# Moving a recurrence channel's gate-weight load behind its first four weight tiles in SP's transfer queue

## What is computed

```python
def even_layer(x, norm_pre, norm_post, w_in, conv_w, conv_b, gate_w, gate_b, lam, sc_w, w_out):
    h = rmsnorm(x, norm_pre)
    proj = h @ w_in
    xa, za, xb, gb, gc, zb = jnp.split(
        proj, [RG_WIDTH, 2 * RG_WIDTH, 2 * RG_WIDTH + SC_WIDTH,
               2 * RG_WIDTH + 2 * SC_WIDTH, 2 * RG_WIDTH + 3 * SC_WIDTH], axis=-1)
    ua = centred_dwconv(xa, conv_w, RG_CONV_LEFT) + conv_b
    ya = rg_lru(ua, gate_w[0], gate_b[0], lam[0], False) + rg_lru(ua, gate_w[1], gate_b[1], lam[1], True)
    ya = ya * jax.nn.silu(za.astype(jnp.float32))
    yb = gb * centred_dwconv(gc * xb, sc_w, SC_CONV_LEFT)
    yb = yb * jax.nn.silu(zb)
    y = jnp.concatenate([ya, yb.astype(jnp.float32)], axis=-1) @ w_out
    return (x + rmsnorm(y, norm_post)).astype(x.dtype)
```

## Time and profile before

| | us |
|---|---|
| median of 3 runs | 2751.83 |
| lowest, highest run | 2749.63, 2751.89 |
| the profiled execution | 2754.38 |
| its span | 2752.2 |

### The profile page before, as it was taken

How to read it: one execution, slowest core, us unless ns; L and a number is a source line. 1 busy time by engine, 2 the same in 40 slices (tenths; PEclk the granted TensorE clock), 3 DMA queues, 4 the chain that set the end, 5 groups by cost and what they waited for, 6 DMA issues and landing times.

```text
span 2752.2 us, 35968 instructions
## 1 busy us (share of the span) xinstructions
PE 2713.7 (99%) x13142; PEld 2170.6 (79%) x13142; DVE 1348.9 (49%) x1609; ACT 712.8 (26%) x1231; POOL 1622.8 (59%) x947
## 2 busy tenths in 40 slices
PE   9999999999999999999999999999999999999999
PEld 6777777867888888867888888788888766788887
DVE  7888824573531461176441444642246777543142
ACT  4443422343200110184210113410012477211010
POOL 4666755513665666602666666566566788566565
PEclk9999999999999999999999999999999999999999
DMA  5322222202332333301332332433232100233232
GB/s 179 100 95 89 91 92 88 81 16 70 97 113 80 98 94 93 97 9 39 93 113 84 92 107 84 130 98 110 83 100 90 55 2 2 85 93 120 77 96 87
DMA packets 62027, 235.57 MB, mean 86 GB/s; under 512 B 6880, under 2 KB 7008, under 8 KB 61792
## 3 DMA queue, kind: packets, MB, share of 16 engines
q1 hardware_dynamic: 61920, 234.14, 27.0%
HBM read 232.02 MB, written 2.10 MB: 85 GB/s over the span
## 4 chain that ended last, share of the span: by engine, by line
PE 82%; DVE 5%; POOL 3%; PEld 3%; ACT 2%; issue 2%; DVEq 1%; PEldq 0%; DMA 0%; POOLq 0%; ACTq 0%; SPq 0%
PE ps L363 23%; PE ps L365 23%; PE ps L364 23%; POOL arena L2412 3%; PE ps L387 1%; PE ps L382 1%; PE ps L381 1%; PE ps L1032 1%; PEld ps L707 1%; PEld ps L708 1%; PEld ps L709 1%; PE ps L1016 1%; PE ps L1202 1%; PE ps L659 0%; PE ps L1225 0%
## 5 line engine op out<-in xcount | busy, mean ns | idle before, releaser
L333 POOL TENSOR_TENSOR w_lo<-ring,w_hi 128x1024 fp32r<-128x1024 f32 (+2 forms) x383 | 990.8, 2587 | 56.0 <-issue 1.5
L331 POOL CAST w_hi<-ring 128x1024 fp32r<-128x1024 f32 (+2 forms) x383 | 435.9, 1138 | 915.3 <-PE ps L365 734.0
L363 PE MATMUL ps<-hi,w_hi 128*128 128x512 f32 x2064 | 809.9, 392 | 5.6 <-POOL w_lo L333 3.5
L365 PE MATMUL ps<-hi,w_lo 128*128 128x512 f32 x2064 | 804.0, 390 | 0.0
L364 PE MATMUL ps<-lo,w_hi 128*128 128x512 f32 x2064 | 803.9, 389 | 0.0
L363 PEld LDWEIGHTS ps<-hi,w_hi 128*128 128x128 f32 x2064 | 387.9, 188 | 93.0 <-POOL w_lo L333 4.9
L364 PEld LDWEIGHTS ps<-lo,w_hi 128*128 128x128 f32 x2064 | 387.8, 188 | 82.3 <-issue 2.4
L365 PEld LDWEIGHTS ps<-hi,w_lo 128*128 128x128 f32 x2064 | 387.9, 188 | 81.0
L363 PE MATMUL ps<-hid_hi,w_hi 128*128 128x512 f32 x704 | 274.3, 390 | 0.0
L364 PE MATMUL ps<-hid_lo,w_hi 128*128 128x512 f32 x704 | 273.9, 389 | 0.0
L365 PE MATMUL ps<-hid_hi,w_lo 128*128 128x512 f32 x704 | 273.9, 389 | 0.0
(11 more groups left out here) (363 smaller groups left out, 3344.4 us busy)
## 6 DMA issues: line engine op xcount, KB each, us to landing
ring<-in_ffn_in SPq DMA_DIRECT2D x176, 512.0 KB, 3.6
ring<-in_even_in SPq DMA_DIRECT2D x48, 512.0 KB, 4.9
ring<-in_ffn_out SPq DMA_DIRECT2D x32, 768.0 KB, 4.2
ring<-in_ffn_out SPq DMA_DIRECT2D x32, 640.0 KB, 3.9
ring<-in_even_out SPq DMA_DIRECT2D x16, 512.0 KB, 3.6
ring<-in_sb_qk SPq DMA_DIRECT2D x12, 512.0 KB, 3.7
ring<-in_odd_v SPq DMA_DIRECT2D x8, 512.0 KB, 3.5
ring<-in_odd_r SPq DMA_DIRECT2D x8, 512.0 KB, 3.6
```

Of the source, the lines that this page charges most:

```text
L331: nc.gpsimd.tensor_copy(high[:, j % 2, 0:cols], ring[:, j, 0:cols])
L333: nc.gpsimd.tensor_tensor(low[:, j % 2, 0:cols], ring[:, j, 0:cols], high[:, j % 2, 0:cols].bitcast(F32), ALU.subtract).then_inc(sem["w_re ...
L363: nc.tensor.matmul(bank, w_hi[:, j % 2, w], x_hi[:, k, :], start=(k == 0), stop=False)
L365: mm = nc.tensor.matmul(bank, w_lo[:, j % 2, w], x_hi[:, k, :], start=False, stop=(k == kt - 1))
```

## The change

In the loop over channels 2 to 7, SP's wait for channel c-2 and the load of the gate weights move from ahead of the channel's first weight tile to behind its fourth (`RING` is 4). The number of instructions, the tiles, the buffers and the conditions of every load stay as they are; only their order in SP's stream is another. From the loop on, line numbers above L610 are one higher in the changed file.

```diff
                     with sp.Fori(0, RG_HEADS // 2 - 1) as i:
                         for jj in range(2):
 
-                            sp.wait_ge(sem["even_channel_done"], 2 * i + (jj + 3))
-                            gate_weight(i + 1, jj)
                             for n in range(6):
+                                if n == RING:
+                                    sp.wait_ge(sem["even_channel_done"], 2 * i + (jj + 3))
+                                    gate_weight(i + 1, jj)
                                 s = 6 * jj + n
                                 sp.wait_ge(sem["w_ready"], 12 * i + (s + 13))
                                 even_weight(i + 1, s)
```

## The result

| | kernel before | changed kernel |
|---|---|---|
| median, us | 2751.12 | 2754.93 |
| lowest, highest, us | 2747.50, 2753.33 | 2753.52, 2756.34 |
| span of the profiled execution, us | 2752.2 | 2753.4 |

Both medians are of 20 runs. The changed kernel takes 3.8 us more; the ratio is 1.0014 with a 95% interval of 1.0008 to 1.0020. The forecast was 2754.8 us. It is a loss of 0.14%, inside the 0.2% that was called "no change", though with this many runs its sign is plain.

A forecast was written before the change was run, and what follows sets the result against it. PE, busy for 99% of the span, bounds the kernel, so gains come only where it stands still or runs slowly. 5.27 - 1.5 - 1.0 + 0.2 = +3.0 us on 2751.83 gives 2754.8 us, range 2748.0 to 2758.8.

The forecast's parts named there:

- The queue block on SP: Weight tiles queued behind SP's wait for DVE; PE's disturbed channels lose 4.83 us together, which moving the wait removes.
- The collision at channel 1: POOL's early split of channel 2's tile 0 blocks DVE's chain to channel 1's `ua`; gate block +5.27 us.
- Channel 1 to 2: Distance between these gate blocks falls from 39.90 to 38.4 us, -1.5, with slow clock taken at 2.3.
- The give-back later: Channels 5 to 6 and 6 to 7 give back their delays of 0.45 and 0.59 us: -1.0.
- The later `ua`: At channels 2 to 7 POOL's cast meets DVE's multiply-adds, leaving `ua` barely in time: +0.2 us, bounds 0 to 1.8.
- Rival 2: Same lock makes `ua` late at each of channels 2 to 7, if POOL's cast begins first: 2759.3 us, +0.27%; 10%.
- Rival 1: Channel 2's early split misses DVE's chain or the chain has slack; pauses go unreplaced: -4.8, 2747.0 us; 18%.
- Rival 3: The change does nothing, since POOL is held by something other than SP's order: 2751.8 us; 4%.

The follow-up runs named there:

- e7: Kernel before, SP's old order, with DVE making channel 1's `ua` inside channel 0 ahead of the scans: 2753.43 us against 2751.07.
- e3: Changed kernel, with POOL's split of channel 2's first tile also waiting for channel 1's `ua`: 2746.85 us against 2751.74 for the kernel before.
- e4: Kernel before, SP's order untouched, with an extra POOL cast and subtraction on constants ahead of channel 2's first split: 2751.65 us against 2751.74.
- e5: Changed kernel, with 30 small matmuls on PE ahead of its wait for channel 1's `ua`: 2753.72 us against 2751.07 for the kernel before.
- e1: Kernel before, with SP's changed order for channel 2 alone, channels 3 to 7 keeping the old order: 2755.18 us against 2751.74.
- b1: Kernel before, unchanged, profiled again: 2750.61 us in a single run.
- b3: Kernel before, unchanged, profiled once more: 2749.30 us in a single run.
- b2: Kernel before, unchanged, profiled once more: 2751.13 us in a single run.
- a1: Changed kernel, unchanged, profiled again: 2753.77 us in a single run.
- e2: Kernel before, with SP's changed order for channels 3 to 7 alone, channel 2 keeping the old order: 2750.09 us against 2751.74.
- e6: Changed kernel, with DVE making channel 1's `ua` inside channel 0 ahead of the scans: 2747.22 us against 2751.07 for the kernel before.

## Why the prediction was right, step by step

**The queue block on SP.** Read rightly. Without it the channels follow each other every 36.11 us (changed kernel), and in e7, where channel 0 ends later, PE's wait before channel 2 grows from 1.88 to 4.50 us.

**The collision at channel 1.** The forecast ran on the clock of the first trace; the changed kernel's stood 0.28 us later from channel 0 on (53.06 for 52.78). Cast of tile 0 at 79.77, read 80.12; L1814's end 84.29, read 84.61; start of the multiply-adds 84.91, read 85.22; their time 5.0, read 4.94; gate block +5.27, read 90.21 - 84.88 = +5.33, or +5.05 without the 0.28. The 0.2 us too much is the step from `ua` to the gate block: 0.20 was taken, and it was 0.05 (90.16 to 90.21). In the kernel before, the 0.22 from 84.66 to 84.88 were PE's last products, so they were slack and not a signal's time. e3 and e4 show the cause, by taking it away and by making it alone.

**Channel 1 to 2.** 38.4 was forecast and 38.71 read; the slow clock was taken at 2.3 and cost 2.5 (e5). That the two are so close is luck. The 2.3 rests on the half clock ending at 94.8, as in the first trace of before, and nothing ties the two ends together: in the changed kernel the half clock lasted 6.8 us where it had lasted 3.4, and part of it fell into the pause. With the same pause it cost 1.6 us in a second execution (37.75) and 3.2 in e1 (39.28). The bounds of 0 to 3.4 hold all three.

**The give-back later.** 1.0 us forecast; 5 to 6 and 6 to 7 fell from 36.56 and 36.70 to 36.11 and 36.12. But the first trace of before had more of these delays than most: over its four executions, channels 2 to 7 were 0.6 us longer than in the changed kernel, not 1.0.

**The later `ua`.** 0.2 us was taken and none was lost. The pattern was there. DVE's and POOL's rows before channel 4's gate block, which began at 201.14:

```profile
195.77 5.00 DVE L1760 SCALAR_TENSOR_TENSOR arena<-arena 128x512 f32<-128x512 f32 x3
```

```profile
196.04 1.38 POOL L331 CAST w_hi<-ring 128x1024 fp32r<-128x1024 f32 x1 [1.43 <-PE ps L365]
```

The cast comes 0.27 us behind the first multiply-add, as worked out, and `ua` is ready at 200.77, 0.37 ahead. Rival 2 thus stayed 0.25 to 0.34 us away at each of the six channels; the profile does not show what would push it over.

**The sum.** +3.0 was forecast. The medians say +3.8 and the traces +3.5 (means of four executions of before and two of the changed kernel, us):

| term | forecast | traces |
|---|---|---|
| channel 0 to 1 | +5.27 | +4.99 |
| channel 1 to 2 | -1.5 | -0.85 |
| channels 2 to 7 (give-back and later `ua`) | -0.8 | -0.60 |
| sum | +3.0 | +3.5 |

The largest miss is the second row. The prediction said that a spell of slow clock can fall differently from run to run, but it booked the one behind the 2 us pause as a fixed part of the kernel before. That spell is there in two of four executions, so the old pause was worth 3.0 us on average and not the 3.79 that were booked. That the forecast of 2754.8 lies 0.1 us from the measured 2754.93 is luck: it was built on a median of three runs, 0.7 us above the 2751.12 of twenty, and its change was 0.8 too small.

The two first traces alone do not give the sum. Their 0 to 7 differs by 2.83 us and the gate block of channel 7 by 3.11 (309.49 for 306.38), but the spans by 1.2 only. Behind channel 7, before's trace has two spells of half clock, near 1265 and 2184 us, that the changed one's has not; the change does not touch that part.

**Rival 1** had the right reading of SP and would have been right with the hold of e3: -4.8 was its price, -4.9 is what e3 measured. That match is in part luck too, since 1.7 of the 4.8 were the slow clock that is not always there: by the traces, e3's 0 to 7 is 4.2 us below the first of before and 3.0 below the mean of four. **Rival 3** falls with the first row of SP.

**Where the channels begin.** The gate block of channel 0 begins anywhere from 51.35 to 53.61 us over these traces. It goes with PE's granted clock from 5 to 25 us: 1.00 in the five traces that begin by 51.72 (b1, b3, e4, e5, e7), 0.91 in the six from 52.78 to 53.29 (before, changed, b2, a1, e1, e2), 0.83 in the two latest (e3, e6). A mean of 0.91 over these 20 us is 3.6 us at half speed. No experiment varied this. It is not the change, since the kernel before is in the first group and in the second; this is why the distances are compared and not the times.

What stays open: why the clock falls in one execution and not in the next, and why the small waits for POOL come at other channels each time.

## What to carry to other kernels

Work that is freed on one engine starts at another moment, and that moment has to be checked against every engine that shares something with it: here POOL's split, over 5 us earlier than needed (80.12 against the 85.93 of e3), fell on a DVE chain with 0.2 us of slack. When a transfer is moved ahead, walk through the new start of its consumer operation by operation against the neighbour's timeline; the rows of the old trace, taken where the two already meet, gave the moments of channel 1's collision to 0.3 us. Where the collision is in the way, hold the freed work behind the tight chain or take the tight operation out of it: both turned a loss of 3.8 us into a gain of 3.9 to 4.9.

## What the runs showed of the hardware

- POOL's cast and subtraction and DVE's operations on two SBUF tiles did not run side by side: DVE's operation of 0.69 us took 2.73 and ended 0.55 us after the subtraction, three multiply-adds of 0.8 took 4.9 to 5.1 at each channel of the changed kernel, and the 2.73 came also when POOL read constants (e4). The Trainium skill, SBUF — State Buffer, section "Who interferes with whom", says that a VectorE instruction with two SBUF inputs contends with a GpSimd instruction that reads SBUF, and that the lock is exclusive. These rows agree.
- After one and the same pause of PE (1.86 to 1.90 us idle), the granted clock fell to half in two executions of five (the first trace of before and b1) and stayed full in three (b2, b3, e2). After an unfilled pause of 4.5 to 5 us it fell in every trace that had one (the changed kernel twice, e1, e7), and also after the one of 2.34 us in e4; where small matmuls filled it (e5), it did not. After the changed kernel's pause of 4.8 to 4.9 us the slow clock cost from 1.6 to 3.2 us (a1, the first trace, e1).
- Half clock that falls where PE has to wait in any case cost nothing: in e4 the gate block took 5.40 us instead of 3.6, and only 0.23 us of waiting was left behind it.
